# Two tables of expert sums in place of one, and a read-back of the first while the last expert runs

## The chip, the cores and the metric

The kernel runs on one core of a Trainium2 chip. The metric is the device time of one execution in microseconds (us), as the median of the runs; the kernel before was run three times. Engines are named as the profile names them: PE does matmuls, DVE, ACT and POOL do elementwise work, SP issues direct transfers, and POOL also issues the indirect ones (rows picked by a list of row numbers).

## The reference

One transformer-like layer on 512 tokens of width 1024: a mixing sub-layer (mLSTM heads and sparse attention), then a mixture-of-experts sub-layer. The change touches the end of the second one:

```python
def body(y, args):                      # once per block of one expert's tokens
    tok_b, g_b, e_b = args
    xb = hf[tok_b]                      # gather the expert's tokens
    u = jax.nn.silu(xb @ w_gate[e_b]) * (xb @ w_up[e_b])
    yb = (u @ w_down[e_b]) * g_b[:, None]
    return y.at[tok_b].add(yb), None    # add rows into the sum

shared = (jax.nn.silu(hf @ ws_gate) * (hf @ ws_up)) @ ws_down
x = x + gt2 * rms_norm(routed + shared, g_ffn_post[l])
```

There are 64 experts of width 256, each token goes to 8 of them, so an expert has 64 tokens on average. All is float32.

## The kernel before

The expert stage (`stage_experts`) walks through the 64 experts in order; every engine runs its own program of steps, one step per expert, in a loop of eight unrolled steps (`turns`, 8 turns, the last one written out). An expert's weights are three matrices of 1 MB. SP loads gate and up into a ring of four places, four experts ahead, as soon as DVE has split the last user of the place (`s_wlo`), and down into two places, two experts ahead, as soon as PE has finished the down product (`s_dn`). In SP's program the down load of expert e+2 stands ahead of the gate and up loads of expert e+5.

For expert e, POOL gathers up to 128 token rows of 4 KB from DRAM into one of four buffers (L1475, `xg`; the fourth is called `rows`), PE transposes them (L1751), multiplies with gate and up (L1761, in three passes of high and low parts, which ACT and DVE make at L1599 and L1681), and after the activation with down (L1815). ACT and DVE scale the product by the gate and write it to `yb`, one half each (L1648, L1732), in one of two buffers by the parity of e. POOL then adds the rows to the table `y_rows` in DRAM (L1481, an indirect transfer that adds; called scatter below).

PE's order in step e is: gate and up of e+1, finding the rows of e+4, transposing the tokens of e+2, the down product of e, transposing u of e+1. POOL's order in step e is: the gather of e+4, which waits until PE has transposed expert e out of that buffer, and then the scatter of e, which waits for both halves of `yb` of e and (L1583) for all scatters before it, since two additions to the same row must not overlap. The write of `yb` of e waits until the scatter of e-2 has landed (L1647, L1731). The number of rows of a transfer is picked by branches over the expert's count (`by_size`), so POOL's loop body is long: some 900 rows of code.

Before the first expert the shared expert's output is stored to `y_rows` (L1623) and its padding rows are set (L1549). After the last one all engines meet, a block for experts with more than 128 tokens is entered and found empty here, and `stage_final` reads `y_rows` back in four pieces (L1980), computes the norm and adds (ACT L1996 and L1998, DVE L2005 to L2013, POOL L1990), and stores.

Of the kernel before, what the change touches and what calls it, by code (L numbers as in the profile page):

```python
# [21 lines left out]
P = 128  # L22
# [1404 lines left out]
def stage_experts(nc, A, G):  # L1427

    with ExitStack() as own:
# [48 lines left out]

        def add_rows(pool, slot, n, rows=CAP):

            return pool.indirect_dma_start(out=G.y_rows, out_offset=bass.IndirectOffsetOnAxis(ap=sidx[0:rows, n:n + 1], axis=0),  # L1481
                                           in_=yb[0:rows, slot, :], in_offset=None, compute_op=ALU.add)


# [2 lines left out]
        with ExitStack() as inner:  # L1487
            def isem(name):
                return inner.enter_context(nc.semaphore(name))
# [17 lines left out]
            s_dn = isem("down_done")  # L1507
            s_ya = isem("y_low_ready")
            s_yd = isem("y_high_ready")
            s_sc = isem("scattered")  # L1510
            s_passed = isem("pool_waits_passed")
            s_zero = isem("xg_zero")
            s_sdn = isem("shared_down_done")
# [13 lines left out]
            @block.sync  # L1527
            def _(sp):

                load_down(sp, 1, 1, s_wd[1])  # L1530
                load_gate_up(sp, 3, 3, s_wgu[3])

                def step(t, n, ahead):
                    e = UNROLL * t + n
                    if ahead(RING):
                        sp.wait_ge(s_wlo, 2 * e + 2)
                        load_gate_up(sp, UNROLL * t + (n + RING), n % RING, s_wgu[n % RING])
                    if ahead(2):
                        sp.wait_ge(s_dn, e + 1)
                        load_down(sp, UNROLL * t + (n + 2), n % 2, s_wd[n % 2])  # L1540

                turns(sp, step)

            @block.gpsimd
            def _(pool):
                for n in range(RING - 1):
                    nc.gpsimd.memset(xg[n], 0.0).then_inc(s_zero, 1)
                for n in range(2):
                    pool.dma_start(G.y_rows[SEQ + n * 64:SEQ + (n + 1) * 64, :], G.xt[0:64, 0, :]).then_inc(s_sc, 16)  # L1549
                for n in range(AHEAD):  # L1550
                    if n == RING - 1:
                        pool.wait_ge(s_sdn, NT)
                        nc.gpsimd.memset(xg[n], 0.0).then_inc(s_zero, 1)
                    pool.wait_ge(s_zero, n + 1)
                    pool.wait_ge(s_idx, n + 1)
                    gather_rows(pool, n, n).then_inc(s_g[n], 16)
                pool.wait_ge(s_yw, 16 * NT)

                def by_size(count, sizes, move):

                    if len(sizes) == 1:
                        move(sizes[0])
                        return
                    half = len(sizes) // 2
                    with pool.If(count > sizes[half - 1]):
                        by_size(count, sizes[half:], move)
                    with pool.Else():
                        by_size(count, sizes[:half], move)

                def count_of(e):  # L1570
                    return pool.value_load(G.count_tab[0:1, bass.ds(e, 1)], min_val=0, max_val=SEQ)

                def step(t, n, ahead):
                    e = UNROLL * t + n
                    if ahead(AHEAD):
                        pool.wait_ge(s_idx, e + AHEAD + 1)
                        pool.wait_ge(s_xp, e + 1)
                        pool.sem_inc(s_passed, 1)
                        count = count_of(e + AHEAD)
                        by_size(count, SIZES, lambda rows: gather_rows(pool, n % RING, (n + AHEAD) % UNROLL, rows).then_inc(s_g[n % RING], 16))  # L1580
                    pool.wait_ge(s_ya, e + 2)
                    pool.wait_ge(s_yd, e + 2)
                    pool.wait_ge(s_sc, 16 * e + 32)  # L1583
                    pool.sem_inc(s_passed, 1)
                    count = count_of(e)
                    by_size(count, SIZES, lambda rows: add_rows(pool, n % 2, n, rows).then_inc(s_sc, 16))

                turns(pool, step)
                pool.wait_ge(s_sc, 16 * E_N + 32)

            @block.scalar
            def _(act):
# [25 lines left out]
                def store_shared(i):  # L1618
                    act.wait_ge(s_sdn, i + 1)
                    nc.scalar.activation(ysh[i].rearrange("p (a b) -> p a b", a=2), ps[:, 4 + 2 * (i % 2):6 + 2 * (i % 2), :],  # L1620
                                         ACT.Copy).then_inc(s_sdc, 1)
                    act.wait_ge(s_sdc, i + 1)
                    act.dma_start(G.y_rows[i * P:(i + 1) * P, :], ysh[i]).then_inc(s_yw, 16)  # L1623

                high_half(0, 0, 0)
                high_half(0, 0, 1)
# [10 lines left out]
                def step(t, n, ahead):  # L1637
                    e = UNROLL * t + n
                    if ahead(2):
                        high_half(t, n + 2, 0)  # L1640
                    if ahead(1):
                        silu(t, n + 1)
                    if ahead(2):
                        x_high(t, n + 2)
                        high_half(t, n + 2, 1)
                    act.wait_ge(s_dn, e + 1)
                    act.wait_ge(s_sc, 16 * e + 16)  # L1647
                    nc.scalar.activation(yb[:, n % 2, 0:512], ps[0:CAP, 4, :], ACT.Copy,  # L1648
                                         scale=found[:, n, 1:2]).then_inc(s_ya, 1)

                turns(act, step)

            @block.vector
            def _(dve):
# [62 lines left out]
                def step(t, n, ahead):  # L1717
# [10 lines left out]
                    if ahead(AHEAD + 1):  # L1728
                        build_pick(UNROLL * t + (n + AHEAD + 1), (n + AHEAD + 1) % 2)
                    dve.wait_ge(s_dn, e + 1)  # L1730
                    dve.wait_ge(s_sc, 16 * e + 16)  # L1731
                    nc.vector.tensor_scalar(yb[:, n % 2, 512:D], ps[0:CAP, 5, :], found[:, n, 1:2], None, ALU.mult).then_inc(s_yd, 1)  # L1732
                    if ahead(1):
                        copy_uT(UNROLL * t + (n + 1), (n + 1) % 2)

                turns(dve, step)

            @block.tensor
# [85 lines left out]
        with ExitStack() as inner:  # L1824
# [38 lines left out]
            def _(pool):  # L1863
                def body(j):
                    pool.wait_ge(s_idx, j + 1)
                    pool.sem_inc(s_passed, 1)
                    gather_rows(pool, 0, 0).then_inc(s_g, 16)
                    pool.wait_ge(s_ya, j + 1)
                    pool.wait_ge(s_yd, j + 1)
                    pool.sem_inc(s_passed, 1)  # L1870
                    pool.indirect_dma_start(out=G.y_rows, out_offset=bass.IndirectOffsetOnAxis(ap=sidx[:, 0:1], axis=0),
                                            in_=yb[:, 0, :], in_offset=None, compute_op=ALU.add).then_inc(s_sc, 16)
                    pool.wait_ge(s_sc, 16 * j + 16)
                    pool.sem_inc(s_added, 1)
# [82 lines left out]
def stage_final(nc, A, G):  # L1957

    with ExitStack() as own:
# [9 lines left out]
        ss = sb("ss_final", [P, NT])  # L1969
        rt = sb("rt_final", [P, NT])  # L1970
        s_in = [sem(f"y_landed{i}") for i in range(NT)]
        s_sq, s_ms, s_rt, s_o, s_out = sem("y_squares"), sem("y_mean_square"), sem("y_root"), [sem(f"out_ready{i}") for i in range(NT)], sem("out_stored")
        s_y = sem("y_normed")
        dch = sem("dve_chain")
# [2 lines left out]
        @block.sync  # L1977
        def _(sp):
            for i in range(NT):
                sp.dma_start(y[:, i, :], G.y_rows[i * P:(i + 1) * P, :]).then_inc(s_in[i], 16)  # L1980
            for i in range(NT):
                sp.wait_ge(s_o[i], 1)
                sp.dma_start(G.out[0, i * P:(i + 1) * P, :], xt[:, i, :]).then_inc(s_out, 16)
# [8 lines left out]
        @block.scalar  # L1992
        def _(act):
            for i in range(NT):
                act.wait_ge(s_in[i], 16)
                nc.scalar.activation(sq[:, i % 2, :], y[:, i, :], ACT.Square, accum_out=ss[:, i:i + 1]).then_inc(s_sq, 1)  # L1996
                act.wait_ge(s_ms, i + 1)
                nc.scalar.activation(rt[:, i:i + 1], ss[:, i:i + 1], ACT.Sqrt).then_inc(s_rt, 1)  # L1998
# [1 line left out]
        @block.vector  # L2000
        def _(dve):
            step = Chain(dve, dch)
            for i in range(NT):
                dve.wait_ge(s_sq, i + 1)
                nc.vector.tensor_scalar(ss[:, i:i + 1], ss[:, i:i + 1], 1.0 / D, EPS, ALU.mult, ALU.add).then_inc(s_ms, 1)  # L2005
                dve.wait_ge(s_rt, i + 1)
# [13 lines left out]
def build(nc, A, out):  # L2020
    with ExitStack() as ctx:
        def sb(name, shape, dt=F32):
# [10 lines left out]
        G.s_roped = ctx.enter_context(nc.semaphore("attention_rotated"))  # L2033
        G.s_wgu = [ctx.enter_context(nc.semaphore(f"gate_up_landed{n}")) for n in range(RING)]
        G.s_wd = [ctx.enter_context(nc.semaphore(f"down_landed{n}")) for n in range(2)]
        G.s_wout = ctx.enter_context(nc.semaphore("w_out_landed"))

        G.w_shared_down = G.maskb[:, :, :].rearrange("p i t -> p (i t)").rearrange("p (f n) -> p f n", f=FC)
# [4 lines left out]
        G.count_tab = sb("expert_counts", [1, E_N], I32)  # L2043
        G.extra_tab = sb("extra_tab", [1, P + 1], I32)
        G.h2_rows = nc.dram_tensor("h2_rows", (SEQ, D), F32, kind="Internal").ap()
        G.y_rows = nc.dram_tensor("y_rows", (SEQ + P, D), F32, kind="Internal").ap()
        G.out = out


# [3 lines left out]
        G.nat = G.main[:, 0:G.QKC].rearrange("p (i n) -> p i n", i=NT)  # L2053
        G.qkc = G.main[:, G.QKC:].rearrange("p (c t) -> p c t", c=2 * HEADS)
        G.wout = G.side[:, 0:8192].rearrange("p (f n) -> p f n", f=2 * HEADS)
        G.w_gate_up = [t.rearrange("p (m c f) -> p m c f", m=2, c=KC)
                       for t in (G.side[:, 0:4096], G.side[:, 4096:8192], G.main[:, 0:4096], G.main[:, 4096:8192])]
        G.w_down = [t.rearrange("p (f n) -> p f n", f=FC) for t in (G.side[:, 8192:10240], G.main[:, G.QKC:G.QKC + 2048])]
# [29 lines left out]
```

## Time and profile before

| what | value |
|---|---|
| runs | 1206.0, 1214.04, 1221.95 us; median 1214.04 |
| profiled execution | 1208.86 us, span 1207.1 us |
| PE busy | 1042.1 us (86%) |
| DVE, ACT, POOL busy | 839.6, 529.2, 349.0 us |
| mean granted PE clock | 0.933 |
| moved by DMA | 298.19 MB, mean 247 GB/s |

The span is the time from the first to the last instruction. The expert stage is by far its longest part. The busy shares are means over stages with different limits; what decides about the change has to be read inside the expert stage and in the last 30 us.

### The profile page before, as it was taken

How to read it: one execution, taken by the hardware profiler on the slowest of the kernel's cores; microseconds unless marked ns; L12 is line 12 of the kernel's file. 1: busy time of each engine (PE TensorE's matmuls, PEld its weight loads, DVE VectorE, ACT ScalarE, POOL GpSimd, SP SyncE). 2: the span in 40 equal slices, each digit the busy share in tenths (PEclk: the TensorE clock that was granted, in tenths of full speed). 3: DMA queues.
4: the chain of work that ended last, by engine and by line, in shares of the span. 5: the costliest groups of instructions: out<-in, count | busy, mean ns of one | idle time of the engine just before them, and what ended most of it. 6: DMA issues, size and time to landing. Idle time of an engine off the chain costs nothing. (4 is left out here: it accounts for less than half of the span.)

```text
span 1207.1 us, 15733 instructions
## 1 busy us (share of the span) xinstructions
PE 1042.1 (86%) x4777; PEld 742.4 (62%) x4778; DVE 839.6 (70%) x1421; ACT 529.2 (44%) x615; POOL 349.0 (29%) x192
## 2 busy tenths in 40 slices
PE   1799997678899979999999699999799997999850
PEld 1696986636744735676666466666566665666630
DVE  4786999956524284888777588778588886678623
ACT  3323354245412115555554455555455554555412
POOL 1351495100000020543312343322443322332311
PEclk9796999868999889999999899999899999999995
DMA  9673343140041634999999699999799999899834
GB/s 363 227 246 105 106 153 129 56 171 1 4 181 51 263 139 153 328 361 344 342 358 346 235 349 369 327 344 356 250 347 346 356 361 351 253 350 367 269 70 151
DMA packets 74087, 298.19 MB, mean 247 GB/s; under 512 B 8917, under 2 KB 21249, under 8 KB 57353
## 3 DMA queue, kind: packets, MB, share of 16 engines
q1 hardware_dynamic: 60096, 259.10, 58.2%
q0 software_dynamic: 12384, 35.18, 12.6%
q10 hardware_dynamic: 1514, 2.97, 0.7%
q14 instruction: 72, 0.59, 0.1%
q8 instruction: 21, 0.34, 0.1%
HBM read 274.71 MB, written 24.67 MB: 248 GB/s over the span
## 5 line engine op out<-in xcount | busy, mean ns | idle before, releaser
L1481 POOL DMA_INDIRECT y_rows<-yb,row_numbers x64 | 125.2, 1956 | 361.5 <-issue 336.1
L1681 DVE TENSOR_TENSOR w_gate_up_lo<-side,w_gate_up_hi 128x2048 fp32r<-128x2048 f32 x64 | 146.7, 2294 | 63.7 <-ACT w_gate_up_hi L1599 63.6
L1681 DVE TENSOR_TENSOR w_gate_up_lo<-main,w_gate_up_hi 128x2048 fp32r<-128x2048 f32 x64 | 146.9, 2295 | 58.5 <-ACT w_gate_up_hi L1599 58.5
L1599 ACT ACTIVATE w_gate_up_hi<-main 128x2048 fp32r<-128x2048 f32 x64 | 122.2, 1909 | 54.2 <-PE ps L1761 54.2
L1761 PE MATMUL ps<-w_gate_up_hi,xT_hi 128*128 128x512 f32 x512 | 143.7, 402 | 2.0 <-DVE xT_lo L1685 1.9
L1599 ACT ACTIVATE w_gate_up_hi<-side 128x2048 fp32r<-128x2048 f32 x64 | 122.0, 1908 | 48.7 <-PE ps L1761 46.7
L1761 PE MATMUL ps<-w_gate_up_hi,xT_lo 128*128 128x512 f32 x512 | 137.5, 390 | 0.0
L1761 PE MATMUL ps<-w_gate_up_lo,xT_hi 128*128 128x512 f32 x512 | 137.0, 389 | 0.0
L1815 PE MATMUL ps<-side,uT 128*128 128x512 f32 x256 | 118.0, 604 | 0.0
L1815 PE MATMUL ps<-main,uT 128*128 128x512 f32 x256 | 115.2, 593 | 1.0 <-DVE uT L1694 1.0
L1475 POOL DMA_INDIRECT xg<-h_rows,row_numbers x48 | 81.4, 1695 | 103.4 <-issue 70.2
L1761 PEld LDWEIGHTS ps<-w_gate_up_hi,xT_lo 128*128 128x128 f32 x512 | 96.1, 188 | 21.2
L1761 PEld LDWEIGHTS ps<-w_gate_up_lo,xT_hi 128*128 128x128 f32 x512 | 96.1, 188 | 20.5
L1685 DVE TENSOR_TENSOR xT_lo<-ps,xT_hi 128x1024 fp32r<-128x1024 f32 x64 | 78.0, 1219 | 43.5 <-ACT xT_hi L1607 43.5
L1761 PEld LDWEIGHTS ps<-w_gate_up_hi,xT_hi 128*128 128x128 f32 x512 | 91.4, 188 | 19.0 <-issue 3.3
L1607 ACT ACTIVATE xT_hi<-ps 128x1024 fp32r<-128x1024 f32 x64 | 65.5, 1023 | 80.6 <-PE ps L1751 80.2
L1648 ACT ACTIVATE yb<-ps,found 128x512 f32<-128x512 f32 x64 | 44.1, 690 | 110.4 <-DMA y_rows<-yb,row_numbers 71.2
L292 POOL TENSOR_TENSOR w_lo<-side,w_hi 128x2112 fp32r<-128x2112 f32 (+3 forms) x12 | 58.3, 4856 | 108.1 <-ACT w_hi L376 107.9
L1751 PE MATMUL ps<-consts,xg 128*128 128x128 f32 x384 | 56.9, 293 | 33.5 <-DMA xg<-h_rows,row_numbers 33.5
L1815 PEld LDWEIGHTS ps<-side,uT 128*128 128x128 f32 x256 | 47.7, 197 | 47.7 <-issue 47.6
L1815 PEld LDWEIGHTS ps<-main,uT 128*128 128x128 f32 x256 | 46.2, 191 | 47.1 <-issue 47.1
L1751 PEld LDWEIGHTS ps<-consts,xg 128*128 128x128 f32 x384 | 48.3, 194 | 35.2 <-DMA xg<-h_rows,row_numbers 34.7
(286 smaller groups left out, 1596.2 us busy)
## 6 DMA issues: line engine op xcount, KB each, us to landing
side<-in_w_exp_gate SPq DMA_DIRECT2D x32, 1024.0 KB, 10.4
side<-in_w_exp_up SPq DMA_DIRECT2D x32, 1024.0 KB, 15.4
side<-in_w_exp_down SPq DMA_DIRECT2D x32, 1024.0 KB
main<-in_w_exp_gate SPq DMA_DIRECT2D x32, 1024.0 KB, 10.9
main<-in_w_exp_up SPq DMA_DIRECT2D x32, 1024.0 KB, 15.5
main<-in_w_exp_down SPq DMA_DIRECT2D x32, 1024.0 KB, 10.1
side<-in_w_ada SPq DMA_DIRECT2D x24, 1024.0 KB, 6.7
side<-in_w_in SPq DMA_DIRECT2D x5, 1056.0 KB, 5.5
```

The costliest lines, as they stand in the source:

```text
L292: nc.gpsimd.tensor_tensor(wlo[:, m % 2, 0:n], stage[:, place[ITEMS[m]] % SLOTS, 0:n], whi[:, m % 2, 0:n].bitcast(F32), ALU.subtract).then_ ...
L1475: return pool.indirect_dma_start(out=xg[slot][0:rows, :], out_offset=None, in_=G.h2_rows, in_offset=bass.IndirectOffsetOnAxis(ap=sidx[0:ro ...
L1481: return pool.indirect_dma_start(out=G.y_rows, out_offset=bass.IndirectOffsetOnAxis(ap=sidx[0:rows, n:n + 1], axis=0), in_=yb[0:rows, slot ...
L1599: nc.scalar.activation(whi[:, half], wgu[n % RING][:, :, HALF * half:HALF * (half + 1), :] .rearrange("p m c f -> p c m f"), ACT.Copy).the ...
L1607: nc.scalar.activation(xhi[:, :, :], ps[:, 0:2, :].rearrange("p b (c t) -> p (b c) t", t=P)[:, :, 0:CAP], ACT.Copy).then_inc(s_xhi, 1)
L1648: nc.scalar.activation(yb[:, n % 2, 0:512], ps[0:CAP, 4, :], ACT.Copy, scale=found[:, n, 1:2]).then_inc(s_ya, 1)
L1681: nc.vector.tensor_tensor(wlo[:, half], src, whi[:, half].bitcast(F32), ALU.subtract).then_inc(s_wlo, 1)
L1685: nc.vector.tensor_tensor(xlo[:, :, :], ps[:, 0:2, :].rearrange("p b (c t) -> p (b c) t", t=P)[:, :, 0:CAP], xhi[:, :, :].bitcast(F32), AL ...
L1751: ins = nc.tensor.transpose(ps[:, c // 4, (c % 4) * P:(c % 4) * P + CAP], xg[n % RING][:, c:D:KC], ident[0:CAP, 0:CAP])
L1761: ins = nc.tensor.matmul(ps[0:CAP, 2 + slot, :], xp[:, HALF * half + c, :], wp[:, half, c].rearrange("p m f -> p (m f)"), start=half == 0 ...
L1815: ins = nc.tensor.matmul(ps[0:CAP, 4 + half, :], uT[:, n % 2, f, :], wd[n % 2][:, f, 512 * half:512 * (half + 1)], start=f == 0, stop=f == ...
```

## The change

There are now two tables, `y_sums[0]` for even and `y_sums[1]` for odd experts, each with its own semaphore (`s_sc[0]`, `s_sc[1]`). The scatter of e waits only for the scatters of its own parity, that is for e-2. The even table starts with the shared expert's output as before; the odd one is set to zero by four transfers of 512 KB from a buffer that POOL clears, which SP issues in the stage's first microseconds. Behind its last load SP waits for the last even scatter (expert 62) and reads the even table into SBUF, while expert 63 is worked on. `stage_final` reads the odd table where it read the only one, and DVE adds the two, piece by piece, before the rest of the norm.

```diff
-            return pool.indirect_dma_start(out=G.y_rows, out_offset=bass.IndirectOffsetOnAxis(ap=sidx[0:rows, n:n + 1], axis=0),
+            return pool.indirect_dma_start(out=G.y_sums[slot], out_offset=bass.IndirectOffsetOnAxis(ap=sidx[0:rows, n:n + 1], axis=0),
...
-            s_sc = isem("scattered")
+            s_sc = [isem("scattered_even"), isem("scattered_odd")]
+            SC0 = 2 * 16
...
                 load_gate_up(sp, 3, 3, s_wgu[3])
+                sp.wait_ge(s_yz, 1)
+                for i in range(NT):
+                    sp.dma_start(G.y_sums[1][i * P:(i + 1) * P, :], yb[:, 1, :]).then_inc(s_yzd, 16)
...
                 turns(sp, step)
+                sp.wait_ge(s_wlo, 2 * (E_N - 2))
+                sp.wait_ge(s_sc[0], SC0 + 16 * (E_N // 2))
+                for i in range(NT):
+                    sp.dma_start(G.y_even[:, i, :], G.y_sums[0][i * P:(i + 1) * P, :]).then_inc(G.s_y_even[i], 16)
...
+                nc.gpsimd.memset(yb[:, 1, :], 0.0).then_inc(s_yz, 1)
                 for n in range(RING - 1):
                     nc.gpsimd.memset(xg[n], 0.0).then_inc(s_zero, 1)
...
-                    pool.wait_ge(s_sc, 16 * e + 32)
+                    pool.wait_ge(s_sc[n % 2], SC0 + 16 * (UNROLL // 2 * t + n // 2))
...
                     act.wait_ge(s_dn, e + 1)
-                    act.wait_ge(s_sc, 16 * e + 16)
+                    act.wait_ge(s_sc[n % 2], SC0 + 16 * (UNROLL // 2 * t + n // 2))
...
-                sp.dma_start(y[:, i, :], G.y_rows[i * P:(i + 1) * P, :]).then_inc(s_in[i], 16)
+                sp.dma_start(y[:, i, :], G.y_sums[1][i * P:(i + 1) * P, :]).then_inc(s_in[i], 16)
...
-                act.wait_ge(s_in[i], 16)
+                act.wait_ge(s_sum, i + 1)
...
+            def add_sums(i):
+                dve.wait_ge(s_in[i], 16)
+                dve.wait_ge(G.s_y_even[i], 16)
+                nc.vector.tensor_tensor(y[:, i, :], y[:, i, :], G.y_even[:, i, :], ALU.add).then_inc(s_sum, 1)
+
+            add_sums(0)
             for i in range(NT):
+                if i + 1 < NT:
+                    add_sums(i + 1)
```

On SP, at the end of the expert stage, four issues stand now behind the last two down loads. In brackets stands what a row waits for.

```order
 L1463 DMA side<-in_w_exp_down 128x2x1024 [waits down_done]
 L1463 DMA main<-in_w_exp_down 128x2x1024 [waits down_done]
+L1552 DMA side<-y_rows_even 128x1024 [waits scattered_even,w_low_half]
+L1552 DMA side<-y_rows_even 128x1024 x3
 L1487 UNCONDITIONAL_BRANCH
```

Nothing else on SP is behind them in this stage; its next row is the branch into the next block.

On DVE, in `stage_final`, the program now begins so (`side` is the even table's copy, `main` the odd one's):

```order
L2024 TENSOR_TENSOR main<-main,side 128x1024 [waits y_even_landed0,in_w_hi_ready]
L2024 TENSOR_TENSOR main<-main,side 128x1024 [waits y_even_landed1,in_h_lo]
L2031 TENSOR_SCALAR ss_final<-ss_final 128x1 [waits in_mod_ready]
L2033 RECIPROCAL rt_final<-rt_final 128x1 [waits in_cols_copied]
L2034 SCALAR_TENSOR_TENSOR main<-main,rt_final,rows 128x1024 [waits in_pool_chain]
L2024 TENSOR_TENSOR main<-main,side 128x1024 [waits y_even_landed2,in_h_hi]
L2031 TENSOR_SCALAR ss_final<-ss_final 128x1 [waits in_mod_ready]
```

Each piece i has got one addition, issued one piece ahead of the norm, and the first two stand ahead of everything else. Semaphores are reused between stages, so their names here are those of an earlier stage. Line numbers in the changed kernel are larger than before: the scale and store of `yb` is at L1662 (ACT) and L1747 (DVE), the scatter stays at L1481.

## Rows read from the trace of the kernel before

**Rows 1.** Who waited for whom, 479 to 1150 us: total, times, longest (us).
```profile
ACT yb L1648 <- DMA y_rows<-yb,row_numbers: 71.2, 20, 5.5
PE ps L1751 <- DMA xg<-h_rows,row_numbers: 33.5, 9, 9.8
```

**Rows 2.** A stretch: length, busy and count of PE, PEld, DVE, ACT, POOL, clock, DMA share, GB/s.
```profile
493.00:536.20 43.20, 43.20 (x197) 30.31 (x196) 35.46 (x57) 23.95 (x21) 21.47 (x9) 1.00 1.02 347
```

**Rows 3.** Timeline of PE, down products of experts 0, 9 and 61: start, length.
```profile
479.08 3.60 PE L1815 MATMUL ps<-side,uT 128*128 128x512 f32 x8
...
571.07 3.60 PE L1815 MATMUL ps<-main,uT 128*128 128x512 f32 x8
...
1149.43 3.60 PE L1815 MATMUL ps<-main,uT 128*128 128x512 f32 x8
```

**Rows 4.** Timeline, 644 to 677 us, a stretch behind a turn's end.
```profile
644.18 1.63 POOL L1481 DMA_INDIRECT y_rows<-yb,row_numbers  x1 [6.56 <-issue]
...
654.08 0.69 ACT L1648 ACTIVATE yb<-ps,found 128x512 f32<-128x512 f32 x1 [5.53 <-DMA y_rows<-yb,row_numbers]
...
655.99 1.52 POOL L1481 DMA_INDIRECT y_rows<-yb,row_numbers  x1 [7.90 <-issue]
...
667.24 2.75 POOL L1475 DMA_INDIRECT xg<-h_rows,row_numbers  x1 [9.73 <-issue]
...
677.02 1.97 PE L1751 MATMUL ps<-consts,xg 128*128 128x128 f32 x8 [9.78 <-DMA xg<-h_rows,row_numbers]
```

**Rows 5.** Timeline, undisturbed: `yb` and scatter of expert 1, gather and transposes of 6.
```profile
493.04 0.69 ACT L1648 ACTIVATE yb<-ps,found 128x512 f32<-128x512 f32 x1 [0.70 <-PE ps L1815]
...
498.72 2.80 POOL L1481 DMA_INDIRECT y_rows<-yb,row_numbers  x1 [3.17 <-issue]
...
502.62 0.98 POOL L1475 DMA_INDIRECT xg<-h_rows,row_numbers  x1 [1.10 <-issue]
...
519.00 1.14 PE L1751 MATMUL ps<-consts,xg 128*128 128x128 f32 x8
```

**Rows 6.** Line L1475 (gathers), whole span: issue to landing.
```profile
DMA to landing us min/median/max: 4.5/9.2/13.0
```

**Rows 7.** DMA issues of the down weights: count, KB each, median us to landing.
```profile
main<-in_w_exp_down SPq DMA_DIRECT2D x32, 1024.0 KB, 10.1
```

**Rows 8.** DMA queues, 490 to 665 us: packets, MB, share of 16 engines.
```profile
q1 hardware_dynamic: 9271, 52.00, 80.1%
q0 software_dynamic: 3070, 8.84, 21.2%
```

**Rows 9.** DMA queues, 868 to 1010 us.
```profile
q1 hardware_dynamic: 7654, 42.97, 81.3%
```

**Rows 10.** Line L1463 (down loads): landing in 480:500, in 860:880, in 1000:1020.
```profile
DMA to landing us min/median/max: 5.9/5.9/5.9
...
DMA to landing us min/median/max: 8.5/8.5/8.5
...
DMA to landing us min/median/max: 17.6/17.6/17.6
```

**Rows 11.** Timeline, expert 63: its `yb` on DVE and its scatter.
```profile
1167.11 0.75 DVE L1732 TENSOR_SCALAR yb<-ps,found 128x512 f32<-128x512 f32 x1 [3.81 <-PE ps L1815]
...
1176.27 1.41 POOL L1481 DMA_INDIRECT y_rows<-yb,row_numbers  x1 [5.23 <-issue]
```

**Rows 12.** Timeline of DVE in the final stage.
```profile
1191.42 1.28 DVE L2008 SCALAR_TENSOR_TENSOR main<-main,rt_final,rows 128x1024 f32<-128x1024 f32 x1
...
1193.23 2.98 DVE L2008 SCALAR_TENSOR_TENSOR main<-main,rt_final,rows 128x1024 f32<-128x1024 f32 x1
...
1199.76 1.23 DVE L2013 TENSOR_TENSOR xt<-xt,main 128x1024 f32<-128x1024 f32 x1
```

**Rows 13.** Timeline, start of the stage: first gather on POOL, first transposes on PE.
```profile
444.55 1.14 POOL L1475 DMA_INDIRECT xg<-h_rows,row_numbers  x1 [0.68 <-DVE row_numbers L1471]
...
459.07 1.04 PE L1751 MATMUL ps<-consts,xg 128*128 128x128 f32 x8
```

More of the change, by code:

```diff
@@ L1509, in stage_experts @@
             s_yd = isem("y_high_ready")
-            s_sc = isem("scattered")
+            s_sc = [isem("scattered_even"), isem("scattered_odd")]
+            SC0 = 2 * 16
+            s_yz = isem("y_zero_tile")
+            s_yzd = isem("y_odd_zeroed")
             s_passed = isem("pool_waits_passed")
@@ L1548, in _ @@
                 for n in range(2):
-                    pool.dma_start(G.y_rows[SEQ + n * 64:SEQ + (n + 1) * 64, :], G.xt[0:64, 0, :]).then_inc(s_sc, 16)
+                    for p in range(2):
+                        pool.dma_start(G.y_sums[p][SEQ + n * 64:SEQ + (n + 1) * 64, :], G.xt[0:64, 0, :]).then_inc(s_sc[p], 16)
                 for n in range(AHEAD):
@@ L1557, in _ @@
                 pool.wait_ge(s_yw, 16 * NT)
+                pool.wait_ge(s_yzd, 16 * NT)
                 def by_size(count, sizes, move):
@@ L1582, in step @@
                     pool.wait_ge(s_yd, e + 2)
-                    pool.wait_ge(s_sc, 16 * e + 32)
+                    pool.wait_ge(s_sc[n % 2], SC0 + 16 * (UNROLL // 2 * t + n // 2))
                     pool.sem_inc(s_passed, 1)
                     count = count_of(e)
-                    by_size(count, SIZES, lambda rows: add_rows(pool, n % 2, n, rows).then_inc(s_sc, 16))
+                    by_size(count, SIZES, lambda rows: add_rows(pool, n % 2, n, rows).then_inc(s_sc[n % 2], 16))
                 turns(pool, step)
-                pool.wait_ge(s_sc, 16 * E_N + 32)
+                for p in range(2):
+                    pool.wait_ge(s_sc[p], SC0 + 16 * (E_N // 2))
             @block.scalar
@@ L1622, in store_shared @@
                     act.wait_ge(s_sdc, i + 1)
-                    act.dma_start(G.y_rows[i * P:(i + 1) * P, :], ysh[i]).then_inc(s_yw, 16)
+                    act.dma_start(G.y_sums[0][i * P:(i + 1) * P, :], ysh[i]).then_inc(s_yw, 16)
                 high_half(0, 0, 0)
@@ L1646, in step @@
                     act.wait_ge(s_dn, e + 1)
-                    act.wait_ge(s_sc, 16 * e + 16)
+                    act.wait_ge(s_sc[n % 2], SC0 + 16 * (UNROLL // 2 * t + n // 2))
                     nc.scalar.activation(yb[:, n % 2, 0:512], ps[0:CAP, 4, :], ACT.Copy,
                                          scale=found[:, n, 1:2]).then_inc(s_ya, 1)
+                act.wait_ge(s_yzd, 16 * NT)
                 turns(act, step)
@@ L1730, in step @@
                     dve.wait_ge(s_dn, e + 1)
-                    dve.wait_ge(s_sc, 16 * e + 16)
+                    dve.wait_ge(s_sc[n % 2], SC0 + 16 * (UNROLL // 2 * t + n // 2))
                     nc.vector.tensor_scalar(yb[:, n % 2, 512:D], ps[0:CAP, 5, :], found[:, n, 1:2], None, ALU.mult).then_inc(s_yd, 1)
@@ L1734, in step @@
                         copy_uT(UNROLL * t + (n + 1), (n + 1) % 2)
+                dve.wait_ge(s_yzd, 16 * NT)
                 turns(dve, step)
@@ L1870, in body @@
                     pool.sem_inc(s_passed, 1)
-                    pool.indirect_dma_start(out=G.y_rows, out_offset=bass.IndirectOffsetOnAxis(ap=sidx[:, 0:1], axis=0),
+                    pool.indirect_dma_start(out=G.y_sums[1], out_offset=bass.IndirectOffsetOnAxis(ap=sidx[:, 0:1], axis=0),
                                             in_=yb[:, 0, :], in_offset=None, compute_op=ALU.add).then_inc(s_sc, 16)
@@ L1971, in stage_final @@
         s_in = [sem(f"y_landed{i}") for i in range(NT)]
+        s_sum = sem("y_summed")
         s_sq, s_ms, s_rt, s_o, s_out = sem("y_squares"), sem("y_mean_square"), sem("y_root"), [sem(f"out_ready{i}") for i in range(NT)], sem("out_stored")
@@ L2035, in build @@
         G.s_wd = [ctx.enter_context(nc.semaphore(f"down_landed{n}")) for n in range(2)]
+        G.s_y_even = [ctx.enter_context(nc.semaphore(f"y_even_landed{i}")) for i in range(NT)]
         G.s_wout = ctx.enter_context(nc.semaphore("w_out_landed"))
@@ L2045, in build @@
         G.h2_rows = nc.dram_tensor("h2_rows", (SEQ, D), F32, kind="Internal").ap()
-        G.y_rows = nc.dram_tensor("y_rows", (SEQ + P, D), F32, kind="Internal").ap()
+        G.y_sums = [nc.dram_tensor(f"y_rows_{name}", (SEQ + P, D), F32, kind="Internal").ap() for name in ("even", "odd")]
         G.out = out
@@ L2055, in build @@
         G.wout = G.side[:, 0:8192].rearrange("p (f n) -> p f n", f=2 * HEADS)
+        G.y_even = G.side[:, 4096:8192].rearrange("p (i d) -> p i d", i=NT)
         G.w_gate_up = [t.rearrange("p (m c f) -> p m c f", m=2, c=KC)
```

## The prediction

> **What bounds the kernel now.** I read the waits of the expert stage first, then its stretches, then the timeline of POOL beside PE, and the DMA queues last. An expert costs PE 10.22 us where nothing is in its way: from the down product of expert 0 to that of expert 9 (479.08 to 571.07) there are nine steps of 10.22 us [rows 3]. From expert 0 to 61 the trace has 1149.43 - 479.08 = 670.35 us, 10.99 per expert; 61 steps of 10.22 would be 623.4. So 47 us of this stage are not PE's work. In an undisturbed stretch PE is busy throughout at full clock (1.00) [rows 2], so the loss lies in single places.
>
> The waits name two things [rows 1]: PE waits 33.5 us for gathers in 9 places, and ACT waits 71.2 us, 20 times, for a scatter before it may write `yb`. Both come from one chain. In [rows 4] a scatter goes out at 644.18; it has landed at 654.08, for at that moment the waiting `yb` is written; the next scatter goes out at 655.99. That is 9.9 us of transfer and 1.9 us of POOL's issue, 11.8 per expert, more than PE's 10.22. While this chain holds, POOL drops behind by over 1 us per expert, and since every gather stands in POOL's program behind a scatter, the gathers get late too. The second ingredient is a hole: at each of the loop's turn ends the first gather comes late (9.73 us idle before it, against 1.10 at an ordinary one) [rows 4, 5]. A POOL on time has 519.00 - 502.62 = 16.4 us from gather to use [rows 5], against a landing of 9.2 us, 13.0 at most [rows 6]. A hole takes 8.6 us of that, and the chain gives POOL no way to recover; the next hole meets a POOL that is already late and PE stands 9.78 us for it [rows 4].
>
> **What the change removes: the wait of a scatter for its neighbour.** A chain now has one scatter in two experts, so it asks for 11.8 / 2 = 5.9 us per expert, far under PE's pace. A scatter goes out 1.9 us behind the start of its `yb`. The write of `yb` waits, as before, for the scatter two back; that one goes out 20.4 - 1.9 = 18.5 us earlier and lands in time by the landing of 9.9 us. In the undisturbed stretch the scatter came 5.7 us behind `yb` (493.04 to 498.72) [rows 5]; 3.8 us of it go, and the gather behind it moves up by as much: 20.2 us of room, 11.6 even behind a hole. That covers the median landing, not the longest one; I price what is left at 0 to 2 us for each of six holes, and take 0, for the next paragraph covers it. The holes themselves, six of them, one at each jump back of the loop, stay, since POOL's code is as long as before.
>
> **What is late next: the weights.** The DMA share is already 1.02 in the good stretches [rows 2]. An expert's weights are three loads of 1024 KB, 3.146 MB [rows 7]. The DMA's need per expert I read from the load queue. In 175 us it moved 52.00 MB, 16.5 experts' worth, beside the gathers and scatters of q0: 10.59 us per expert [rows 8]. In 142 us of a later stretch it moved 42.97 MB: 10.40 us [rows 9]. The landing of the down load tells the same from the other side: at PE's pace it grows, from 8.5 to 17.6 us over 14 experts, 0.65 us per expert, which makes 10.9 [rows 10]. So I bound the DMA's need by 10.4 and 10.9 us per expert and take 10.6, the row of the longest stretch. It is above PE's 10.22, so the queue fills: a down load is issued 3.8 us behind the start of a down product (its 3.60 us and the issue) [rows 3], lands in 5.9 us at the stage's start [rows 10], and is due 20.4 us behind that start, 16.6 us after its issue. The room of 10.7 us lasts for 28 experts at 0.38 each; from there on PE waits a little for each down weight. The down product of expert 61 then starts at 483 (479.08 + 3.8, the first such issue) + 59 x 10.6 + 5.9 = 1114.3 instead of 1149.43: **-35.1 us**. With 10.4 it would be 1102.5, where PE's own floor lies too: -47. With 10.9 it is 1132: -17.4. Gather waits that remain behind holes fall inside this shortage: while PE stands, the queue drains.
>
> A rule of the Trainium skill speaks to this. The page "DMA: Bandwidth & Descriptors", section Specifications, gives HBM about 358 GB/s per core. By it, and with the 60.84 MB per 16.5 experts of [rows 8], an expert would need an estimated 10.3 us, and the sum would be -45. The trace has 347 GB/s where the share is 1.02 [rows 2], below the page's figure, so I stay with the measured rate.
>
> **The zeroing and the start.** Four stores of 512 KB on SP behind expert 3's weights, and one more memset and two more padding stores ahead of POOL's first gathers: each of them is shorter than a gather's own issue, 1.14 us, so 3.4 us at most [rows 13]. The first gather is used at 459.07, 14.5 us after its issue, against a landing of 9.2; PE is busy with the shared expert until then. The 2 MB are 6 us of DMA at 347 GB/s in a part where the queue isn't full, and nobody waits for them before the first `yb` at 482. I take 0, with 2 us as the upper end.
>
> **The tail.** Expert 63's `yb` starts at 1167.11 and its scatter goes out at 1176.27, held by that of 62 [rows 11]. Now it goes 1.9 us behind: -7.3 us. The read of the even table (2 MB, 6 us at 347 GB/s) runs beside this scatter and just ahead of the read of the odd one in the same queue: 0 to 6 us. I take +1.5, since the scatter's own landing (4.5 us at least [rows 6]) and the meeting of the engines behind it cover most. In the final stage DVE gets four additions of the size of the one at 1199.76, 1.23 us [rows 12]. The second hides behind ACT's square; three lie on the path. Two of them now meet POOL's additions, but these met a multiply before (2.98 against 1.28 us [rows 12]), which is then free: +3.8 us, between 3.7 and 3 x 2.98 = 8.9. Together **-2.0 us**.
>
> **Sum**: -35.1 - 2.0 = -37.1 us. The profiled execution, 1208.86 us, would become 1172. The median of the runs is 1214.04, 5.2 above it; against it I forecast **1177 us**.
>
> **Rivals.**
> - PE's floor. The DMA keeps up at 10.4 us or less. For it: nine steps in a row hold 10.22 [rows 3]. Against: the growing landings. Result 1214 - 47 - 2 = 1165. Chance 0.15. By the Trainium skill's figure for HBM, weighed above, the time would come out here, an estimated 1167.
> - The load queue is nearly the bound already. At 10.8 to 10.9 us, as the growing landings say [rows 10], the chain's removal brings 17 to 23 us: 1189 to 1195. For it: the present mean is 10.99, close to it. Against: that mean has PE's standstills in it, behind which the queue is short of work. Chance 0.20.
> - The change doesn't release POOL. The gathers are late for the holes alone, and the 33.5 us that PE waits for them [rows 1] stay; only the remaining 13.5 us and the tail go: 1198. Against: at 654.08 it is a scatter's landing that frees both `yb` and the next scatter, with the gather behind them [rows 4]. Chance 0.05.
> - Slower. Two scatters in flight disturb each other or the loads: q0 holds 21.2% of 175 us for 16.5 experts, 2.2 us each [rows 8]. If the overlap raised that price so far that an expert needs 11.2 us, all would be lost; from 11.6 (q0 at 3.2 us) it is 2% slower, 1238, and with q0's price doubled 1309. Against: a scatter lands in 9.9 us and the next goes out 10.2 us later, so they overlap only behind a hole. Chance 0.04. The Trainium skill, page "DMA: Bandwidth & Descriptors", section Queues, rings and completion order, says that an engine takes turns between queues by packet; both scatters are in one queue, so by it the loads would lose no turn, which would leave this rival nearly nothing. No row here shows two in flight.
>
> **Numbers.** The forecast (10.4 to 10.75 us per expert: 1166 to 1187) has 0.56. The range 1162 to 1203 takes in the floor with a run that is a little luckier, and the rival of the loads. About 2%, 24 us, is what a measurement of this kernel tells from no change. Under 1190 lie the forecast, the floor and a small part of the loads' rival: faster 0.73; within 2%: 0.23; slower: 0.04.
>
> **What would show it.** Right: ACT's waits for scatters nearly gone; POOL's scatters about 2 us behind `yb`; PE's stalls of some 9 us gone and its clock at 1.00 throughout the stage; in their place short waits of the down product for `side` or `main` weights in the second half; mean step about 10.6. Wrong: steps of 10.22 without such waits (then the DMA had room), gather waits of several us behind holes (then POOL is still late), or loads landing ever later at a pace over 10.9 (then the overlap costs). In the tail, DVE's additions should start within 4 us of the read of the odd table; if they wait for the even one, that read is the new bound.

## The result, and the profile after

| | before | after |
|---|---|---|
| median of 14 runs each | 1207.43 us | 1201.78 us |
| range | 1199.3 to 1221.95 | 1193.77 to 1204.1 |
| span of the profiled execution | 1207.1 us | 1198.1 us |
| expert 0's down product to expert 61's | 670.35 us | 664.24 us |
| expert 61's down product to the end | 57.7 us | 57.7 us |

The ratio is 0.9947 (95% interval 0.9921 to 0.9973): half a per cent faster. I had forecast 1177 us with a range of 1162 to 1203. The median lies inside the range at its slow end, but the step of 37 us is one of 6.

The timeline of PE, down products of experts 0, 9 and 61, answers to [rows 3]:

```profile
476.20 3.60 PE L1831 MATMUL ps<-side,uT 128*128 128x512 f32 x8
...
568.16 3.60 PE L1831 MATMUL ps<-main,uT 128*128 128x512 f32 x8
...
1140.44 3.60 PE L1831 MATMUL ps<-main,uT 128*128 128x512 f32 x8
```

The first nine steps take 10.22 us each, as before; over 61 steps the mean is 10.89 where it was 10.99. (I don't put the stage's start, 2.9 us earlier, down to the change: it lies between 473 and 481 us in the profiles of this study, with either kernel as the base.)

Who waits for transfers now, 470 to 1140 us (total, times, longest), against [rows 1]:

```profile
ACT w_gate_up_hi L1613 <- DMA side<-in_w_exp_up: 28.9, 10, 3.5
ACT w_gate_up_hi L1613 <- DMA main<-in_w_exp_up: 25.5, 8, 3.9
...
PE ps L1831 <- DMA side<-in_w_exp_down: 14.6, 10, 2.7
...
PE ps L1831 <- DMA main<-in_w_exp_down: 8.5, 9, 2.0
...
PE ps L1767 <- DMA xg<-h_rows,row_numbers: 3.9, 2, 2.1
```

The change did what it says. The 71.2 us in which ACT waited for scatters are gone, the 33.5 us in which PE waited for gathers are 3.9. In their place stand 54.4 us of ACT for up weights and 23.1 us of PE for down weights. Now the same window of the load queue, first before the change, then after it (490 to 1120 us; packets, MB, share of 16 engines):

```profile
q1 hardware_dynamic: 32037, 180.06, 76.7%
q0 software_dynamic: 10702, 30.84, 21.0%
```

```profile
q1 hardware_dynamic: 32234, 180.70, 78.4%
q0 software_dynamic: 10945, 31.56, 21.6%
```

The weights that passed in 630 us are 180.06 and 180.70 MB, 11.01 and 10.97 us per expert. The change took a wait away from a kernel whose weights came no faster. These numbers alone don't say which of the two sets the pace, since SP loads only what PE and DVE have freed; the kernels with fewer bytes below decide it.

### The profile page after: what moved, and what is told of

The parts are those of the page before. It is cut to its first block and busy times, and to the rows that moved or that the text cites. A ratio compares the mean times of both kernels' runs of the same rounds, so it can differ in the third digit from the quotient of the medians.

```text
span 1198.1 us, 15727 instructions
## 1 busy us (share of the span) xinstructions
PE 1043.2 (87%) x4777; PEld 740.0 (62%) x4778; DVE 843.5 (70%) x1425; ACT 530.7 (44%) x615; POOL 410.9 (34%) x195
## 5 line engine op out<-in xcount | busy, mean ns | idle before, releaser
L1475 POOL DMA_INDIRECT xg<-h_rows,row_numbers x48 | 106.7, 2224 | 165.1 <-issue 126.9
L1831 PE MATMUL ps<-side,uT 128*128 128x512 f32 x256 | 122.5, 624 | 14.6 <-DMA side<-in_w_exp_down 14.6
L1481 POOL DMA_INDIRECT y_rows_even<-yb,row_numbers x32 | 75.6, 2363 | 102.4 <-issue 102.4
L1481 POOL DMA_INDIRECT y_rows_odd<-yb,row_numbers x32 | 77.1, 2410 | 90.0 <-issue 90.0
L1831 PEld LDWEIGHTS ps<-main,uT 128*128 128x128 f32 x256 | 46.1, 190 | 57.9 <-issue 47.1
L1662 ACT ACTIVATE yb<-ps,found 128x512 f32<-128x512 f32 x64 | 44.1, 690 | 82.2 <-PE ps L1831 82.2
L1676 DVE TENSOR_SCALAR pick<-consts,place_in_expert 128x128 bf16<-128x128 f32 x256 | 63.3, 323 | 0.7 <-PEq L1106 0.7
```

Of the source, the lines that this page charges most:

```text
L1475: return pool.indirect_dma_start(out=xg[slot][0:rows, :], out_offset=None, in_=G.h2_rows, in_offset=bass.IndirectOffsetOnAxis(ap=sidx[0:ro ...
L1481: return pool.indirect_dma_start(out=G.y_sums[slot], out_offset=bass.IndirectOffsetOnAxis(ap=sidx[0:rows, n:n + 1], axis=0), in_=yb[0:rows ...
L1676: ins = nc.vector.tensor_scalar(pick[:, slot, i, :], k[:, K_IOTA:K_IOTA + CAP], posm[:, bass.ds(NT * e + i, 1)], None, ALU.is_equal)
L1831: ins = nc.tensor.matmul(ps[0:CAP, 4 + half, :], uT[:, n % 2, f, :], wd[n % 2][:, f, 512 * half:512 * (half + 1)], start=f == 0, stop=f == ...
```

## The experiments

Twelve kernels ran on three chips, each beside runs of the kernel before on the same chip. Kernels named `_two` have two chains, `_one` has one. The two `light` kernels, the two `scat` kernels and tail_none leave work out, so their results are not the full ones. "Stage" is the time from expert 0's down product to expert 61's in the profiled execution.

| kernel | median us | ratio to before (95%) | stage us |
|---|---|---|---|
| joined | 1220.74 | 1.0075 (1.0033 to 1.0116) | 685.0 |
| light_one | 1168.42 | 0.9678 (0.9610 to 0.9745) | 630.5 |
| light_two | 1161.54 | 0.9598 (0.9534 to 0.9661) | 622.9 |
| scat16 | 1157.68 | 0.9600 (0.9563 to 0.9636) | 623.7 |
| scat_plain | 1170.37 | 0.9710 (0.9653 to 0.9767) | 631.8 |
| deep_one | 1207.72 | 1.0000 (0.9970 to 1.0030) | 676.5 |
| deep_two | 1191.57 | 0.9856 (0.9792 to 0.9919) | 653.4 |
| wide_two | 1199.19 | 0.9921 (0.9883 to 0.9959) | 664.0 |
| deep_wide_two | 1187.00 | 0.9834 (0.9761 to 0.9906) | 649.4 |
| deep_acc | 1192.41 | 0.9877 (0.9814 to 0.9939) | 656.0 |
| tail_late | 1203.73 | 0.9953 (0.9929 to 0.9977) | 664.5 |
| tail_none | 1192.21 | 0.9888 (0.9824 to 0.9951) | 663.3 |

**Less weight to load: light_one, light_two.** In each, half of every down matrix is left out of the loop:

```diff
-            eng.dma_start(wd[slot], w_down[e].rearrange("(f p) n -> p f n", p=P)).then_inc(s_wd, 16)
+            eng.dma_start(wd[slot][:, 0:1], w_down[e].rearrange("(f p) n -> p f n", p=P)[:, 0:1]).then_inc(s_wd, 16)
```

> The kernel before with half of each down matrix left unloaded in the loop (512 KB less per expert; the sums are then of other numbers). Theory 'loads' (the DMA's rate for weights bounds both kernels at 10.9 us per expert): the DMA needs 9.4 us per expert, below PE's 10.22, and landings get shorter, so the scatter chain shrinks to some 7 + 1.9 us too: the stage comes near PE's floor, 625 to 635 us, the whole at 1165 to 1175. Rival 'chain' (in the kernel before the chain bounds by itself): it stays at 1195 to 1205.

> The changed kernel with half of each down matrix left unloaded in the loop. Theory 'loads': steps at PE's floor of 10.22 us, stage 624 to 628 us against 664, no waits of PE or ACT for weights, the whole 1160 to 1168. Rival (something other than the weights holds it, such as two scatters in flight): waits for weights go but others appear, 1180 or more.

Both went as the theory of the loads says. With two chains the stage is PE's floor: 61 steps of 10.21 us, and PE has no gap from 490 to 1090 us (a part of it, 490 to 610 us, light_two):

```profile
490.00:610.00 120.00, 120.00 (x542) 83.32 (x542) 98.28 (x155) 67.87 (x59) 65.40 (x24) 1.00 0.97 307
```

With one chain 7.6 us more are left, in one late gather and eight waits of `yb` (light_one, waits, 490 to 1090 us):

```profile
ACT yb L1648 <- DMA y_rows<-yb,row_numbers: 15.9, 8, 4.0
...
PE ps L1751 <- DMA xg<-h_rows,row_numbers: 4.6, 1, 4.6
```

So 38 us of the kernel before went away with its single chain intact, as soon as the DMA had 0.5 MB less to carry per expert. In these eight waits the last scatter had gone out 5.2 to 10.4 us before, 8.0 in the median; in the 20 waits of the kernel before it was 6.1 to 12.2, median 9.7. With 1.9 us of POOL's issue the chain comes to 9.9 us, just under PE's 10.22, where it had been above it. The chain was slow because the DMA was full.

**Less to scatter: scat16, scat_plain.** One moves 16 rows per scatter, the other writes rows without adding:

```diff
-                    by_size(count, SIZES, lambda rows: add_rows(pool, n % 2, n, rows).then_inc(s_sc[n % 2], 16))
+                    by_size(count, SIZES, lambda rows: add_rows(pool, n % 2, n, 16).then_inc(s_sc[n % 2], 16))
```

```diff
-                                           in_=yb[0:rows, slot, :], in_offset=None, compute_op=ALU.add)
+                                           in_=yb[0:rows, slot, :], in_offset=None)
```

> The changed kernel with each scatter cut to 16 rows (most additions are left out; all else as before, weights complete). Theory 'loads': what the weights lack is time on the shared DMA engines, and the scatters take about half of q0's 2.4 us per expert; 10.97 falls to about 9.9, below PE's 10.22: stage 624 to 632 us, the whole at 1163 to 1172. Rival 'HBM reads' (the read rate for weights itself is the limit, whatever the scatters do): stage stays over 655, 1192 or more.

> The changed kernel with scatters that write their rows and do not add (the sums are lost; all rows and bytes of weights as before). It prices the addition inside the transfer. If the reading back of the table's rows is what makes the scatters dear: q0's share falls and the whole comes to 1165 to 1180; if a plain write of the rows costs as much: 1195 to 1203.

With all weights loaded, scat16 reaches PE's floor too. So the limit is not the reading of weights by itself but something that weights and rows share. The queue of the indirect transfers shows the price, 490 to 1090 us, in the changed kernel, in scat_plain and in scat16:

```profile
q0 software_dynamic: 10329, 29.86, 21.5%
```

```profile
q0 software_dynamic: 10907, 31.36, 15.5%
```

```profile
q0 software_dynamic: 7475, 19.54, 12.2%
```

The plain writes carry more MB and take 15.5% instead of 21.5%. Per expert (172.40 and 182.19 MB of weights passed meanwhile, 54.8 and 57.9 experts) this is 2.35 us against 1.61: adding in the transfer costs about 0.75 us of all sixteen engines' time per expert, as much as an expert's lack (10.97 - 10.22).

What is shared is left open. It can be the engines' time, or the traffic of the memory: per expert q0 counts 0.54 MB in both kernels, so if an addition first reads its rows back, that is in none of these figures. With some 64 rows of 4 KB more in 10.95 us, the changed kernel's 338 GB/s would be an estimated 362, close to the 357 of scat_plain. No run tells the two apart.

**One part alone: joined.** Both tables, but a scatter waits for both parities again:

```diff
                     pool.wait_ge(s_sc[n % 2], SC0 + 16 * (UNROLL // 2 * t + n // 2))
+                    pool.wait_ge(s_sc[(n + 1) % 2], SC0 + 16 * (UNROLL // 2 * t + (n + 1) // 2))
```

> Two tables as in the change, but a scatter waits again for all scatters before it (both parities). It does one part of the change alone: the second table, its zeroing and its read-back. If the removed wait brought what the stage gained (6 us between the down products of experts 0 and 61), the stage is back at about 670 us and the whole at 1207 to 1211. If the gain came from something else (a luckier start, the tail), it stays at 1202.

It came out slower than either guess: 0.75% above the kernel before, with PE's waits for gathers back (490 to 1120 us):

```profile
PE ps L1768 <- DMA xg<-h_rows,row_numbers: 41.8, 7, 9.6
```

So the second table costs some 9 us where it is not used for a second chain (4 to 14 by the interval), and the second chain is worth the distance from 1.0075 to 0.9947, some 15 us. The change is the sum, -6. Of the 9 us the tail explains 5 to 6 (below). The rest is not settled. In joined's profiled execution, itself 14.8 us longer than that of the kernel before, the stage has 14.7 us more (685.0 against 670.35) and the time behind it 5.2, and the stage starts 5.2 us earlier. One more wait on POOL in a chain that binds again could do it, but no run shows it alone.

**Earlier loads: deep_two, deep_one.** Four places for down weights instead of two, and gate and up issued one expert earlier (core of the edit):

```diff
-                    if ahead(RING):
-                        sp.wait_ge(s_wlo, 2 * e + 2)
-                        load_gate_up(sp, UNROLL * t + (n + RING), n % RING, s_wgu[n % RING])
-                    if ahead(2):
+                    if ahead(RING + 1):
+                        sp.wait_ge(s_wlo, 2 * e + 4)
+                        load_gate_up(sp, UNROLL * t + (n + RING + 1), (n + 1) % RING, s_wgu[(n + 1) % RING])
+                    if ahead(4):
                         sp.wait_ge(s_dn, e + 1)
-                        load_down(sp, UNROLL * t + (n + 2), n % 2, s_wd[n % 2])
+                        load_down(sp, UNROLL * t + (n + 4), n % 4, s_wd[n % 4])
```

> The changed kernel with all its bytes, but loads issued earlier: four places for down weights instead of two (a down load goes out four experts ahead, not two), and gate and up one expert earlier. Theory 'loads' (rate): the mean step stays at 10.8 to 10.9 us, only the waits' places move; gain under 5 us, 1197 to 1203. Rival 'lead' (the rate would do, the loads are issued too late and the queue runs short in each stall): steps of 10.3 to 10.5, 1170 to 1180.

> The kernel before (one table, one chain) with the earlier loads of deep_two. Theory 'loads': the chain's surplus over the load queue is small, but with weights early the chain and the holes are what holds it: stage 665 to 675 as before, whole 1200 to 1210, so that deep_two's gain needs both. Rival: the lead alone does it, 1190 to 1195.

deep_two fell between my two theories (waits, 490 to 1120 us, then the queue, 490 to 1120 and 490 to 1090 us):

```profile
ACT w_gate_up_hi L1619 <- DMA main<-in_w_exp_up: 60.3, 12, 6.9
ACT w_gate_up_hi L1619 <- DMA side<-in_w_exp_up: 55.6, 12, 7.0
```

```profile
q1 hardware_dynamic: 32440, 181.30, 78.3%
...
q1 hardware_dynamic: 31164, 174.83, 79.3%
```

The waits for weights are longer than ever, but later: the first step of PE that late weights lengthen is that of expert 35, at 838 us. The rate is little better. Up to 1120 us it is 10.93 us per expert, but deep_two is almost out of loads by then (the last but one goes out at 1100.80). Up to 1090 us it is 10.80, against 10.95 in the changed kernel (172.40 MB). The difference stands in the first part: 107.59 MB against 105.33 from 490 to 850 us, then 50.62 against 50.99 from 850 to 1030. So the 11 us come from the larger stock at the stage's start and from a queue that runs fuller while the stock lasts; how they divide isn't shown. Once the lead is eaten, the rate is the old one. deep_one has the same lead and gains nothing: the single chain binds instead, with ACT waiting 53.3 us for scatters. So the two edits are worth 1.4% together, nothing (the lead) and 0.5% (the chains) alone.

**Pieces of 8 KB: wide_two, deep_wide_two.**

```diff
-            eng.dma_start(wd[slot], w_down[e].rearrange("(f p) n -> p f n", p=P)).then_inc(s_wd, 16)
+            eng.dma_start(wd[slot], w_down[e].rearrange("(p f) n -> p f n", p=P)).then_inc(s_wd, 16)
...
-                        ins = nc.tensor.transpose(ps[:, 2 + slot, f * P:f * P + CAP], u[:, f * P:(f + 1) * P], ident[0:CAP, 0:CAP])
+                        ins = nc.tensor.transpose(ps[:, 2 + slot, f * P:f * P + CAP], u[:, f:DE:FC], ident[0:CAP, 0:CAP])
```

> The changed kernel, all bytes and the full result, with the down weights laid out so that a partition reads 8 KB in one piece (rows 2p and 2p+1) where it read two pieces of 4 KB; PE transposes every second column of u to match. If the DMA loses time per piece, the load queue gets faster by some 3%: stage about 650 us, the whole 1186 to 1194. If only bytes count: 1199 to 1204, as the change.

> Two chains, early loads and the 8 KB pieces of the down weights together, full result. If the pieces' gain (1199 against 1202, within noise) is real it adds up with deep_two's 1191: 1186 to 1189; if not, 1190 to 1192.

These kernels have a sixth fewer packets in both queues together, but the stage is the same within 0.3 us alone and 4 us shorter on top of the earlier loads; the intervals overlap in both pairs. If there is a gain, it is at most that. deep_wide_two, 1187.0 us, has the lowest median of the kernels that compute everything.

**The tail: tail_late, tail_none, deep_acc.** The even table read in the final stage; not read and not added at all; joined by an adding DMA in place of DVE:

```diff
-                sp.dma_start(y[:, i, :], G.y_sums[1][i * P:(i + 1) * P, :]).then_inc(s_in[i], 16)
...
+                pool.wait_ge(G.s_y_even[i], 16)
+                pool.dma_start(y[:, i, :], G.y_sums[1][i * P:(i + 1) * P, :], accum_op=ALU.add).then_inc(s_in[i], 16)
```

> The changed kernel with the read of the even table put into the final stage, ahead of each piece of the odd one, so that it runs beside nothing. In the change the time from the last scatter's issue to the read-back was 12.4 us against 8.5 before. If the early read is what lengthens it: 8.5 us again here, but the first pieces land later, 3 to 6 us in the final stage; whole within 2 us of 1202 or up to 1206. If the early read hides well: 1206 to 1208.

> The changed kernel without the read of the even table and without the additions (the even sums are left out of the result). From the last scatter to the read-back 8.5 us instead of 12.4, final stage 22.4 instead of 25.1: 1194 to 1197 if the tail gave back what those two say, 6.6 us; 1200 to 1202 if it gave back nothing.

> deep_two with the tables joined by the transfer: POOL reads the odd table with an adding DMA on top of the even one in SBUF, so DVE's four additions go. The prediction priced them at 3.8 us. If the adding read is no slower than SP's: 1187 to 1188; if it is slower by more than the additions: 1192 to 1196.

The last scatter and the read-back, in the changed kernel and in tail_none:

```profile
1160.57 1.42 POOL L1481 DMA_INDIRECT y_rows_odd<-yb,row_numbers  x1 [3.34 <-issue]
1172.97 2.65 SPq L1997 DMA_DIRECT2D main<-y_rows_odd  x4
```

```profile
1159.65 1.42 POOL L1481 DMA_INDIRECT y_rows_odd<-yb,row_numbers  x1 [3.34 <-issue]
...
1168.42 2.63 SPq L1993 DMA_DIRECT2D main<-y_rows_odd  x4
```

12.4 against 8.8 us: the early read lies beside the last scatter, and without it the read-back comes 3.6 us sooner. tail_late has 8.7 there, and pays 28.1 instead of 25.1 us afterwards, so it comes to the same. From the last scatter to the end it is 37.5 us in the changed kernel and 31.9 in tail_none: the second table costs 5.6 us at the end. The medians don't tell the adding DMA from DVE (0.9877 against 0.9856, and the intervals overlap); from expert 61's down product to the end it is 57.6 us with the adding DMA and 59.0 in deep_two, one profile each.

## Why the prediction was wrong

**The bound before: wrong in weight.** I read the scatter chain (11.8 us per expert) as what held the kernel and the load queue as what would come next. The chain was real, but its 9.9 us landing was that of a full DMA. light_one shows it: with lighter loads the same chain lets 40 of the 47 us go. (PE's waits for gathers were a little more than I counted: those for the fourth buffer, `rows`, are another 4.4 us, 3 times.)

**The need of 10.6 us per expert: the step that failed.** The stage should have become 35.1 us shorter and became 6.1. I took the rate from two stretches [rows 8, 9] in which PE ran well, between the standstills. Over the whole stage, 490 to 1120 us, an expert takes 10.97 us now, at a DMA share of 1.00. (The 11.01 before is no need: the share was 0.98, with standstills in it.) The stretch I had chosen was like the changed kernel's first part, 10.67 us per expert up to 750 us (76.67 MB in 260 us); from there to 1120 us it is 11.19 (104.04 MB in 370 us). With 10.97 my own formula gives 483 + 59 x 10.97 + 5.9 = 1136, a gain of 13 us. The bounds of 10.4 and 10.9 didn't hold the value, though the growing landings [rows 10] pointed at 10.9 and I called them a rival.

Why the second part is slower is open, but the runs show what it goes with. From 970 to 1030 us the DMA moved 343, 353 and 354 GB/s in the kernel before, deep_one and joined, which have one chain, 351 in scat_plain, whose two chains only write, and 314 to 336 in the seven kernels with all weights and two adding chains (joined, then the changed kernel; the last two numbers are the DMA share and GB/s):

```profile
970.00:1030.00 60.00, 57.53 (x262) 40.35 (x260) 48.47 (x77) 32.06 (x28) 15.35 (x11) 1.00 1.02 354
```

```profile
970.00:1030.00 60.00, 56.65 (x246) 38.32 (x245) 43.53 (x67) 29.90 (x27) 25.30 (x11) 0.94 1.00 336
```

So a rate read between the standstills of one chain did not hold for two chains without them.

**The room before the shortage: too large.** I had it last for 28 experts. The first down product that waits for its weight is that of expert 16:

```profile
643.88 3.70 PE L1831 MATMUL ps<-side,uT 128*128 128x512 f32 x8 [2.08 <-DMA side<-in_w_exp_down]
```

At 10.97 us the room of 10.7 us would last for 14 experts, so this is partly the same mistake. The other 7 us are not all accounted for. I counted the down load's 16.6 us only. The up load stands behind gate's, and both stand in SP's program behind the wait for a down product; ACT's waits for them are 54.4 us in sum, but how much of that reaches PE isn't shown. The stage is 40.8 us above 61 steps of 10.22. Of these PE's waits are 23.1 us for down weights and 3.9 for gathers, and 6.6 are a loss that I had not priced, PE's clock. Three down products ran slowly: those of experts 44 and 54 took 5.40 us each, behind waits of 1.89 and 2.68 us, and that of expert 50 took 6.56, behind waits of 2.14 and 0.92 us (windows of the changed kernel; its clock is the third number from the end):

```profile
1016.17 6.56 PE L1831 MATMUL ps<-side,uT 128*128 128x512 f32 x8 [0.92 <-DMA side<-in_w_exp_down]
```

```profile
1014.00:1016.00 2.00, 1.16 (x8) 0.97 (x8) 0.48 (x2) 0.72 (x1) 0.00 (x0) 0.78 1.00 344
1016.00:1024.00 8.00, 7.83 (x16) 3.89 (x17) 5.38 (x8) 2.80 (x3) 0.99 (x1) 0.63 0.91 268
```

The granted clock is between its two levels there, 1.2 and 2.4 GHz, and the eight matmuls took 6.56 us instead of 3.60 [rows 3]. But a wait of the same length need not cost this: behind the 2.08 us shown above the product took 3.70 us. I had written that the clock would stay at 1.00; it is 0.99 over the stage.

**The release of the scatters: wrong in size, without effect.** I forecast a scatter 1.9 us behind ACT's `yb`, and 3.8 us of new room for gathers. In the undisturbed stretch it is 5.1:

```profile
490.05 0.69 ACT L1662 ACTIVATE yb<-ps,found 128x512 f32<-128x512 f32 x1 [0.61 <-PE ps L1831]
...
492.46 0.75 DVE L1747 TENSOR_SCALAR yb<-ps,found 128x512 f32<-128x512 f32 x1
...
495.15 3.46 POOL L1481 DMA_INDIRECT y_rows_odd<-yb,row_numbers  x1 [2.50 <-issue]
```

DVE writes its half 2.4 us behind ACT, and the scatter needs both. Only 0.6 us went. All but two gathers were in time all the same: one behind the first hole cost PE 1.8 us, another 2.1.

**The tail: -2.0 forecast, 0.0 measured.** The scatter of expert 63 goes out 6.7 us earlier (7.3 forecast). The early read costs 3.9 us, not 1.5: it does not hide beside the last scatter. The final stage is 2.8 us longer, less than the 3.8. Up to the first multiply it is 1.0 us longer instead of 1.2. From the first to the last multiply it is 1.8 longer instead of 2.5: the additions ran undisturbed beside POOL's, and the two multiplies that I had thought would be free of POOL took 2.76 us, little less than before (2.98 [rows 12]).

```profile
1181.81 1.22 DVE L2024 TENSOR_TENSOR main<-main,side 128x1024 f32<-128x1024 f32 x1
...
1183.56 2.76 DVE L2034 SCALAR_TENSOR_TENSOR main<-main,rt_final,rows 128x1024 f32<-128x1024 f32 x1
```

**The rivals.** What came is the rival of the load queue, to which I gave 0.20, one step further out than I priced it. PE's floor was not reached. The stage moved 338 GB/s on average at a DMA share of 1.00, and scat_plain 357 GB/s with plain writes. The page "DMA: Bandwidth & Descriptors" of the Trainium skill gives 358 GB/s per core (section Specifications). On average the changed kernel's trace stays below it, and scat_plain's mean lies at it, but from 580 to 670 us scat_plain moved 369 GB/s: here the figure is no ceiling. (By it my formula would have given PE's floor, -47 and 1165 us, and not the -45 and 1167 that I wrote.) The slower rival, scatters that disturb each other, did not show in q0's price, which stayed at 2.3 to 2.4 us per expert. As a part of the lower rate late in the stage it is not excluded.

## What to carry to other kernels

A wait for a transfer is only worth its length if the transfer engines have time to spare. A share near 1.0 is a warning and no proof: it was 0.98 over the stage of the kernel before and 0.97 in light_two, where PE never waits. The test is cheap: leave out part of the largest load, in the kernel before, and see whether the chain still holds. When a shared resource is full, an earlier issue buys a stock once, and only fewer bytes, or cheaper ones, buy a rate: here 0.9% for the earlier issue, 2.4% for plain writes and 3.5% for less weight, each on top of two chains.

## What the runs showed that I had not expected

- An adding scatter costs the DMA engines far more than its bytes: q0 held 21.5% of them for 29.86 MB, and 15.5% for 31.36 MB when it wrote only. The plain-writing kernel was some 30 us faster than the changed one; its stage of 631.8 us is 8 above PE's floor.
- Behind waits of 2.14 and 0.92 us close together the clock was 0.63 in the next 8 us, and behind a single wait of 1.89 us a down product took 5.40 us instead of 3.60; most waits of about 2 us cost no clock.
- While PE waited for weights the DMA share stayed near 1.0 (0.97 to 1.03 in stretches of 43 us from 490 to 1092 us) though the rate went from 352 GB/s (619 to 662 us) down to 311 (1006 to 1049). It goes with two chains that add; the mechanism is open.
